# Two chained transformer blocks on one core: modulation chunks at other places, the Fourier sums taken token tile by token tile, first weight chunks in pieces

## The reference

```python
h  = modulate(rmsnorm(x, norm_mix_g[i]), sh1, sc1)       # h * (1 + sc1) + sh1
m  = fourier_mixer(h, w_fourier_out)                     # layer 0: real FFT over tokens and 256 features, then w_o
m  = retention_mixer(h, w_ret_in, w_ret_out, ...)        # layer 1
x  = x + g1 * m
h  = modulate(rmsnorm(x, norm_ffn_g[i]), sh2, sc2)
x  = x + g2 * (silu(h @ w_gate) * (h @ w_up)) @ w_out
...
mod = silu(c) @ w_ada[i] + b_ada[i]                      # gives sh1, sc1, g1, sh2, sc2, g2
out = modulate(rmsnorm(x, final_norm_g), shf, scf)
```

## Time and profile before

| | |
|---|---|
| median of 3 runs | 1191.15 us |
| the profiled execution's own time | 1189.39 us |
| its span, first to last instruction | 1187.2 us |
| mean granted TensorE clock | 0.991 |
| PE, DVE, ACT busy | 1146.8, 851.0, 521.0 us |
| DMA | 259.81 MB, mean 219 GB/s |

### The profile page before, as it was taken

The page is one execution under the profiler, slowest core; times in us unless marked ns, Lnnn a source line. Parts: engine busy times, 40 slices in busy tenths (PEclk is TensorE's granted clock), DMA queues, the critical chain, the costliest instruction groups (busy, mean ns, idle before and its releaser), DMA issues.

```text
span 1187.2 us, 13991 instructions
## 1 busy us (share of the span) xinstructions
PE 1146.8 (97%) x5824; PEld 965.3 (81%) x5824; DVE 851.0 (72%) x1009; ACT 521.0 (44%) x463; POOL 27.4 (2%) x51
## 2 busy tenths in 40 slices
PE   6999999999899999998999999999999999999996
PEld 5898998888688888877778888879976887888885
DVE  5789988986667677575657767478955867767755
ACT  5556555634444344444343434334423433434430
POOL 1000000000000000000000000000001000000000
PEclk8999999999999999999999999999999999999998
DMA  8754563547357768532357777448753563786761
GB/s 310 280 213 163 187 231 130 176 167 269 142 205 258 301 265 316 204 141 72 138 181 272 262 305 290 191 177 320 278 202 122 212 249 142 255 311 259 287 234 36
DMA packets 38638, 259.81 MB, mean 219 GB/s; under 512 B 4144, under 2 KB 6448, under 8 KB 7856
## 3 DMA queue, kind: packets, MB, share of 16 engines
q1 hardware_dynamic: 36960, 251.84, 57.0%
q0 software_dynamic: 1616, 7.08, 1.6%
HBM read 257.86 MB, written 1.05 MB: 218 GB/s over the span
## 4 chain that ended last, share of the span: by engine, by line
PE 85%; DVE 9%; issue 3%; ACT 2%; DMA 1%; POOL 0%; SPq 0%; DVEq 0%; POOLq 0%; ACTq 0%
PE pair L416 41%; PE pair L477 24%; PE pair L442 10%; DVE w_lo L1097 4%; PE tp L495 2%; PE tp L554 2%; DVE hb L1145 2%; PE tp L716 1%; PE tp L668 1%; DMA raw<-stream 1%; ACT w_hi L743 1%; PE tp L581 1%; ACT ht_hi L761 1%; PE tp L694 1%; DVE ht_lo L1157 1%
## 5 line engine op out<-in xcount | busy, mean ns | idle before, releaser
L1097 DVE TENSOR_TENSOR w_lo<-raw,w_hi 128x2048 fp32r<-128x2048 f32 x182 | 412.8, 2288 | 92.8 <-ACT w_hi L743 92.6
L743 ACT ACTIVATE w_hi<-raw 128x2048 fp32r<-128x2048 f32 x182 | 347.6, 1916 | 223.9 <-DMA raw<-stream 133.3
L416 PE MATMUL pair<-w_hi,ht_lo 128*128 128x512 f32 x816 | 327.9, 402 | 20.8 <-DVE w_lo L1097 12.2
L416 PE MATMUL pair<-w_lo,ht_hi 128*128 128x512 f32 x816 | 319.8, 392 | 0.0
L416 PE MATMUL pair<-w_hi,ht_hi 128*128 128x512 f32 x816 | 319.7, 392 | 0.0
L416 PEld LDWEIGHTS pair<-w_hi,ht_lo 128*128 128x128 f32 x816 | 154.3, 189 | 57.6 <-issue 14.7
L416 PEld LDWEIGHTS pair<-w_lo,ht_hi 128*128 128x128 f32 x816 | 154.2, 189 | 33.1
L416 PEld LDWEIGHTS pair<-w_hi,ht_hi 128*128 128x128 f32 x816 | 154.5, 189 | 31.3 <-issue 1.2
L477 PE MATMUL pair<-w_hi,gt_lo 128*128 128x512 f32 x360 | 142.3, 395 | 0.2 <-DVE gt_lo L1163 0.2
L477 PE MATMUL pair<-w_lo,gt_hi 128*128 128x512 f32 x360 | 140.3, 390 | 0.0
L477 PE MATMUL pair<-w_hi,gt_hi 128*128 128x512 f32 x360 | 140.1, 389 | 0.0
(11 more groups left out here) (201 smaller groups left out, 1101.8 us busy)
## 6 DMA issues: line engine op xcount, KB each, us to landing
raw<-stream SPq DMA_DIRECT2D x238, 1024.0 KB, 4.9
xres<-x SPq DMA_DIRECT2D x2, 512.0 KB, 6.8
prow<-rows POOLq DMA_DIRECT2D x1, 1024.0 KB, 9.7
xres<-x POOLq DMA_DIRECT2D x2, 512.0 KB, 4.9
dt<-decay POOLq DMA_DIRECT2D x1, 1024.0 KB, 7.1
outT<-outb SPq DMA_DIRECT2D x4, 256.0 KB, 2.2
csr<-dft POOLq DMA_DIRECT2D x1, 768.0 KB, 4.4
crow<-rows POOLq DMA_DIRECT2D x1, 512.0 KB, 6.4
```

The costliest lines, as they stand in the source:

```text
L416: mm = pe.matmul(pair[use % 2][:, t, :], a[:, 4 * c + k, t * P:(t + 1) * P], b[:, w % WS, k * 512:(k + 1) * 512], start=(c == 0 and k == 0 ...
L743: sc.activation(w_hi[:, w % WS, :], raw[:, n % RAW, :], ACT.Copy).then_inc(hi_done, 1)
L1097: v.tensor_tensor(w_lo[:, w % WS, :], raw[:, n % RAW, :], whi32[:, w % WS, :], ALU.subtract).then_inc(raw_done, 1)
```

## The change

- **Modulation chunks.** `ADA_TICKS`: 0, 1, 2, 5, 17, 18, 20, 31, 33 become 6, 18, 20, 33, 34, 35; in down0 three (1, 3, 5) become six (1 to 6). The total stays 56.
- **Start.** Chunks 0 and 1 are split in four pieces each; chunk 0 is also loaded in four. Tile 1 of x is asked for before the chunk. PE takes zu chunk by chunk, both tiles, in pieces, with 4 more warming products; zv is then an ordinary `wide`. `crow`, `hgrow` and the masks are asked for after chunk 5's hi part; silu(c) and the copy of the masks come later.
- **Normalisations.** DVE scales the first half, ACT the second (four ACTIVATE of 128 x 128 with scale and bias from columns). PE waits for one half at a time. `lo` of one chunk stands between DVE's two halves; at norm1 a chunk's split is drawn ahead of the normalisation.
- **Fourier.** The token sums of tile 0 run as soon as its feature sums are split, those of tile 1 at the end; they add up in `pair` instead of `tp`. The transposes of tile 0 stand in the middle of a chunk of the product ahead (`between`).
- **End.** The columns for the last modulation are made before the last two tiles, whose halves go to DVE and ACT.

```diff
-ADA_TICKS = [0, 1, 2, 5, 17, 18, 20, 31, 33]
-ADA_TICKS += ffn_adas("ffn0") + [W0["down0"] + j for j in (1, 3, 5)]
+ADA_TICKS = [6, 18, 20, 33, 34, 35]
+ADA_TICKS += ffn_adas("ffn0") + [W0["down0"] + j for j in range(1, 7)]
...
-             ("rows0", 2, "row_copied"), ("norm2b", 2, "norm"), ("dft1b", 4, "split"), ("dft2", 4, "split"),
+             ("norm2b", 2, "norm"), ("rows0", 2, "row_copied"), ("dft1b", 4, "split"),
...
+            sp.dma_start(xres[:, 1, :], x[:, 1, :]).then_inc(x_in[1], 16)
             sp.dma_start(col[:], cols).then_inc(small_in, 16)
-            sp.dma_start(raw[:, 0, :], stream[0]).then_inc(landed[0], 16)
-            sp.dma_start(xres[:, 1, :], x[:, 1, :]).then_inc(x_in[1], 16)
+            for q in range(PIECES):
+                sp.dma_start(raw[:, 0, q * 512:(q + 1) * 512], stream[0][:, q * 512:(q + 1) * 512]).then_inc(first_in[q], 16)
...
-                sp.wait_ge(raw_done, n + 1 - RAW)
+                sp.wait_ge(raw_done, pieces_done(n - RAW))
...
-            pool.dma_start(crow[:], rows[4:5, :].to_broadcast([P, D])).then_inc(crow_in, 16)
             rsqrt(RQ["norm0"], 2)
-            pool.wait_ge(hi_done, 2)
...
+            pool.wait_ge(hi_done, pieces_done(5))
+            pool.dma_start(crow[:], rows[4:5, :].to_broadcast([P, D])).then_inc(crow_in, 16)
...
-                wait_split(split, 2)
                 for c in range(4):
                     wait_chunk(w + c)
+                    if c < 2:
+                        wait_split(split, c + 1)
                     if c % 2 == 0:
                         claim_pair(use + c // 2)
                     wide_part(w + c, use + c // 2, c % 2, 0)
                     if c == 2:
                         norm()
-                wait_split(split, 4)
                 for c in range(4):
+                    if c < 2:
+                        wait_split(split, 3 + c)
                     wide_part(w + c, use + c // 2, c % 2, 1)
...
+            def first_tile(t, half, ready, n):
+
+                pe.wait_ge(ready, n)
+                turn(tile_job("norm0", t, half), [xn[:, t, (4 * half + k) * P:(4 * half + k + 1) * P] for k in range(4)])
...
+            def first_part(c, t, after={}):
+
+                n = SPLIT[tile_job("norm0", t, c)] + 1
+                for k in range(4):
+                    piece = PIECES * c + k + 1
+                    if t == 0:
+                        pe.wait_ge(hi_done, piece)
+                    if k == 0:
+                        pe.wait_ge(t_hi, n)
+                    out = pair[USE["zu"] % 2][:, t, :]
+                    ki, tk, wk = 4 * c + k, slice(t * P, (t + 1) * P), slice(k * 512, (k + 1) * 512)
+                    pe.matmul(out, ht[0][:, ki, tk], w_hi[:, c, wk], start=(c == 0 and k == 0), stop=False)
+                    if t == 0:
+                        pe.wait_ge(raw_done, piece)
+                    pe.matmul(out, ht[0][:, ki, tk], w_lo[:, c, wk], start=False, stop=False)
+                    if k == 0:
+                        pe.wait_ge(lo_done, n)
+                    mm = pe.matmul(out, ht[1][:, ki, tk], w_hi[:, c, wk], start=False, stop=(c == 1 and k == 3))
+                    if k in after:
+                        after[k]()
+                if t == TT - 1:
+                    mm.then_inc(w_used, 1)
...
+            first_tile(0, 0, xn_half, 1)
+            keep_warm(4)
+            first_part(0, 0, after={0: next_halves})
+            first_part(0, 1, after={1: lambda: first_tile(1, 1, xn_done, 2)})
+            first_part(1, 0)
+            first_part(1, 1)
+            wide(W0["zv"], USE["zv"])
...
-                  after={(1, 0): turn_tile("tx", xres, 1, x_ready, 4),
-                         (1, 1): turn_tile("norm2", xn, 0, xn_done, 5)})
+                  between={(2, 1): turn_tile("norm2", xn, 0, xn_done, 5)},
+                  after={(1, 0): turn_tile("tx", xres, 1, x_ready, 4)})
...
+            features("dft1", 0)
+            wait_evac(pe, USE["pleg"])
+            wait_evac(pe, USE["pleg"] + 1)
+            tokens("dft1", 0, (0, 1))
+            turn_tile("norm2", xn, 1, xn_done, 6)()
+            tokens("dft1", 0, (2, 3))
+            gate_rows("rows0", 1)
+            wait_split("norm2b", 2)
+            features("dft1b", 1)
+            tokens("dft1b", 1, range(4))
             outer(W0["fo"], 4, USE["fo"], tiles(ht),
...
+            def norm_scaled(name, t, scale, shift, dst, half=1):
+
+                k = tile_job(name, t, half)
+                act.wait_ge(tp_done, k + 1)
+                if k in SPLIT:
+                    at_least(act, lo_done, SPLIT[k] - 1)
+                for m in range(4):
+                    f = 4 * half + m
+                    ins = sc.activation(dst[:, m * P:(m + 1) * P], tp[k % BANKS][:, m * P:(m + 1) * P], ACT.Identity,
+                                        scale=scale[:, f:f + 1], bias=0.0 if shift is None else shift[:, f:f + 1])
+                ins.then_inc(sem(RELEASE[k][0]), 1)
...
             norm_squares(RQ["norm0"], 0, 0)
-            split_hi(0)
-            norm_his("norm0", 0)
-            split_hi(1)
             norm_squares(RQ["norm0"] + 1, 1, 0)
+            for q in range(3):
+                hi_piece(0, q)
+            norm_hi("norm0", 0, 0)
+            hi_piece(0, 3)
+            first_scaled(0)
+            norm_hi("norm0", 1, 0)
+            for q in range(PIECES):
+                hi_piece(1, q)
+            norm_hi("norm0", 0, 1)
+            first_scaled(1)
+            norm_hi("norm0", 1, 1)
             for w in range(2, WS):
                 split_hi(w)
-            act.wait_ge(crow_in, 16)
-            sc.activation(crow[:], crow[:], ACT.Silu).then_inc(ca_done, 1)
-            norm_his("norm0", 1)
...
-                norm_his(name, 0)
+                norm_his(name, 0, scale, shift)
                 tick(w - 1)
...
             for t in range(TT):
                 post_squares(RQ["mix"] + 2 * t, t, w + 3, USE["wout"], 3)
-                if t == 0:
-                    tick(w)
+                tick(w + 2 if t else w)
                 norm_squares(RQ["mix"] + 2 * t + 1, t, 1 + t)
                 tick(w + 3 if t else w + 1)
-                norm_his("norm1", t)
-                if t == 0:
-                    tick(w + 2)
+                norm_his("norm1", t, colv("ffn_pre", 0, 8))
...
-            dft_his("dft1b", 1, range(4))
-            for gr in range(4):
-                k = JOB["dft2"] + gr
-                hi(k, ht[0][:, 2 * gr:2 * gr + 2, :], _two(tp[k % BANKS][:], k))
-                if gr != 2:
-                    tick(w - 2 + (gr + 1) // 2)
-            boundary(W0["fo"] + 3, RQ["norm3"], "norm3", 7)
+                norm_his("norm2", t, moda[:, 0, :], mod[:, 0:8])
+            gate_rows("rows0", grow[0])
+            dft_his("dft1b", 1, (0, 1, 2))
+            tick(w - 2)
+            dft_his("dft1b", 1, (3,))
...
+            def mix_his(groups):
+                for gr in groups:
+                    act.wait_ge(mix_done, gr + 1)
+                    sc.activation(ht[0][:, 2 * gr:2 * gr + 2, :], mixed(gr).rearrange("p (a b) -> p a b", a=2),
+                                  ACT.Copy).then_inc(mix_hi, 1)
+
+            mix_his((0, 1))
+            tick(w - 1)
+            mix_his((2, 3))
+            tick(w)
```

More of the change, by code:

```diff
@@ L146, with tile_job, pieces_done @@
 USE, JOB, RELEASE, SPLIT = plan_psum()
-def tile_job(name, t):
-    return JOB["norm2b"] if name == "norm2" and t else JOB[name] + 2 * t
+def tile_job(name, t, half=0):
+    if name == "norm0":
+        return JOB[name] + 2 * half + t
+    return (JOB["norm2b"] if name == "norm2" and t else JOB[name] + 2 * t) + half
+PIECES = 4
+FINE = 2
+def pieces_done(n):
+    return n + 1 + (PIECES - 1) * min(n + 1, FINE)
 RQ = {}
@@ L257, in program @@
         landed = [sem(f"landed{i}") for i in range(RAW)]
+        first_in = [sem(f"first_in{q}") for q in range(PIECES)]
+        xn_half = sem("xn_half")
         raw_done = sem("raw_done")
@@ L474, in outer @@
                     for half in range(2):
+                        if half and (c, t) in between:
+                            between[c, t]()
                         for k in range(2):
@@ L673, in _ @@
+            features("dft1", 0)
[8 more added lines that the diff above has]
+            tokens("dft1b", 1, range(4))
             outer(W0["fo"], 4, USE["fo"], tiles(ht),
-                  before={(c, 0): lambda c=c: wait_split("dft2", c + 1) for c in range(4)},
+                  before={(c, 0): lambda c=c: pe.wait_ge(mix_lo, max(c + 1, 2)) for c in range(4)},
@@ L916, in boundary @@
                 tick(w)
-                norm_his(name, 1)
+                norm_his(name, 1, scale, shift)
             def gated_chunks(half, name0, plan):
```

244 lines of the change are left out of this document (147 added, 97 removed).

## The result

The changed kernel takes 1176.76 us, median of 4 runs (1175.15 to 1178.84), beside 1190.62 us before in the same comparison (1189.44 to 1191.34): a ratio of 0.9886, 95% interval 0.9864 to 0.9907, so 1.1% faster. Run again beside other kernels it took 1178.01 (1174.04 to 1178.24), ratio 0.9884 (0.9866 to 0.9902). The forecast was 1175.0, with 1173.3 for a profiled execution; the profiled one took 1175.15 (span 1173.1), 14.2 less than before, where 16.1 were forecast.

A forecast was written before the change was run, and what follows sets the result against it. TensorE, busy 97% of the span, bounds the kernel; with the same products only its idle time can change. Terms -6.6 + 6.1 + 2.2 - 4.1 - 6.8 - 6.3 - 0.6 = -16.1 take 1191.15 to 1175.0 us, range 1170 to 1180 (1167 to 1184 with rivals).

The forecast's parts named there:

- down0: Six modulation chunks in a row in down0: chunk 74 ready before needed, so 0 lost, bounds 0 and 5 us.
- the rival, whose mechanism is what happened: down0 stalls too: with landings up to 6.6 us six pairs lose 6.3 less the lead's 1.2, giving 1180; 8%.
- wa and wout: Two modulation chunks ahead of merge(1) make TensorE wait for its tile: 6.1 us lost, bounds 2.5 and 9.
- The clock behind it: Half clock for 3.4 to 5.3 us after the wait at wa: 2.2 us lost, bounds 0 and 2.7.
- The start: Up to qa: first product near 11.2, qa near 36 instead of 42.71, 6.6 us gained, bounds 3 and 8.
- the second rival: Start and clock gains fall short: tile 1 lands late and holds both tiles, half clock lasts longer; 1181, 17%.
- norm1: Joint behind wout: tile 1's products start at 319.0 instead of 323.2, 4.1 us taken as gain, bounds 2.4 and 4.5.
- norm3 to norm5: Three joints, first gap gone and tile 1's products sooner: 2.1 us gained each, 6.3 in all, bounds 1 and 2.6 each.
- Fourier: Fourier stage: token sums of tile 0 fill idle time, fo starts at 552.8, 6.8 us gained, bounds 4 and 7.
- ScalarE's scaling: Second halves scaled on ScalarE: 1.1 us for four, or 1.6 with about 93 ns per column operand.
- the end: After the last transposes, scaling shared by VectorE and ScalarE: 0.6 us gained, bounds 0 and 0.9.

The follow-up runs named there:

- down_spaced: Changed kernel with three modulation chunks in down0 (ticks 1, 3, 5) instead of six in a row, the others at ticks 17, 19, 31: 1175.44 us.
- both_free: Changed kernel with seven modulation chunks before down0, five in it (ticks 1, 3, 4, 5, 6), none at ticks 34 and 35 in wa: 1166.42 us.
- wa_free: Changed kernel with its first six modulation chunks at ticks 6, 17, 18, 20, 31, 33, none at ticks 34 and 35 in wa: 1168.60 us.
- merge_first: Changed kernel with merge(1) one place earlier on VectorE, ahead of the tick that holds the split of chunk 40: 1172.97 us.
- wa_warm: Changed kernel with 18 warming products on TensorE in the stall ahead of the transposes of ga tile 1: 1176.22 us.
- scale_first: Changed kernel with VectorE scaling and splitting tile 0's first half before tile 1's power -1/2 at the start: 1175.67 us.
- crow_early: Changed kernel with crow (512 KB) asked for at once by GpSimd's queue, as before the change: one execution, 1176.59 us.
- dve_scales: Changed kernel with both halves of the scaling on VectorE again in norm1 to norm5: 1179.23 us.

## Why the prediction was right, point by point

- **The total.** 1175.0 forecast, 1176.76 and 1178.01 measured, inside 1170 to 1180. By the medians 13.9 were gained instead of 16.1. In the one execution that was profiled the sum is off by 1.9. One term, down0, makes 1.8 of it. The others are off by 0.2 to 0.6 each, and that they cancel to within 0.2 is luck.
- **down0, the term that failed.** It was put at 0: 5.6 us a pair against 5.45, chunk 74 ready 1.2 before it is needed. That took 4.7 us for every landing, the median of the earlier trace rows. With an item freed every 2.3 us, several loads are under way at once; those asked for at 454.7 to 459.7 took 5.8, 6.3 and 6.8, and the `w_lo` behind them started at 462.42 and 468.44, 7.9 and 6.0 after the one before. The next two pairs took 5.5 and 5.9, their loads 4.7 to 5.0. That this shows at the last chunk lies in `outer` too: it goes through the last four chunks for tile 0 first, 12 products (2.72 us) each, and then for tile 1. By the starts of products and the ends of `w_lo`:

| chunk | `w_lo` ends | TensorE is there | lead |
|---|---|---|---|
| 70 | 456.84 | 467.04 | 10.2 |
| 71 | 464.71 | 472.48 | 7.8 |
| 72 | 470.74 | 475.20 | 4.5 |
| 73 | 476.28 | 477.92 | 1.6 |
| 74 | 482.17 | 480.64 | -1.5 |

  So most of the lead goes in these four, as it did before (11.2 at chunk 71, 3.7 at chunk 74), and 0.15 a chunk does not describe it. The need was forecast rightly (483.7, which is 480.6 here, 3.1 being gained by then); the chunk was ready 2.8 later than forecast. The 6.6 of the earlier trace rows was used only for the rival, whose mechanism is what happened, at 1.8 instead of 5.1. Over the ten profiled executions with six chunks in a row the step was 1.4 to 3.1, never 0, and it was largest (3.1) in the two whose slowest load there took 7.6 and 7.9; among the other eight (6.4 to 7.4, a step of 1.4 to 2.2) there is no clear order. down_spaced and both_free take it away.
- **wa and wout.** Right in kind: 5.5 instead of 6.1, because chunk 40 landed 4.9 after it was asked for, where the prediction took 5.7. wa_free, merge_first and wa_warm show the order, the landing and the clock apart.
- **The clock behind it.** 1.8 instead of 2.2 in the first profile. Over the eight executions with this stall the slow products alone cost 0.7 to 2.1, with the transposes 1.4 to 2.9; four of the eight lie above the term's upper bound of 2.7. By the Trainium skill (TensorE: Matmul & The Clock Gate, What's actually happening) activity is what releases the full rate; wa_warm agrees: warming products, whose results nobody uses, kept it at 1.00.
- **The start.** 6.1 instead of 6.6. First product 11.36 (11.2 forecast), half clock 3.4 us (3 forecast), which cost 1.3 to 1.7 (1.5 to 2 forecast). The cause was split wrongly: crow is worth about 3, not 1.2. That tile 1 would land late and hold tile 0, the second rival, did not happen: it landed at 6.93, and scale_first gains nothing by its order. In crow_early tile 1 and the columns both land 3 us later and the first product with them, so the rival was a real possibility; which of the two held it there is not separated.
- **norm1, norm3 to norm5, Fourier.** 4.3, 2.0 each and 6.5, within 0.3 of the terms. At norm1 the clock happened to stay; in 7 of the 12 profiled executions with that gap it fell, at a cost of 1.4 to 1.6 us. That is one reason why the medians lie above the first profile.
- **ScalarE's scaling, a price that was too low.** Forecast 1.1 us for four with scale and shift. It is 1.1 with a scale alone and 1.5 with both:

```profile
L860 ACT ACTIVATE hb<-tp,mod,moda 128x128 f32<-128x128 f32 x32 | 11.9, 451 | 0.0
L860 ACT ACTIVATE hb<-tp,col 128x128 f32<-128x128 f32 x16 | 4.5, 365 | 2.8 <-PE tp L528 2.8
```

  The forecast took the 592 and 1024 ns of the earlier trace rows as times from start to start; they are the durations of single instructions. By the same line a 128-element one without columns would last 0.27 (an estimate). With a scale from a column it lasts 0.365, with both 0.451: 0.09 for each column operand. The Trainium skill (ScalarE: Activation LUTs, What ACT_TABLE_LOAD costs) has 93 ns for each, and the trace agrees for both. In a row they overlap: 4.5 / 16 is 0.28 from start to start, 11.9 / 32 is 0.37, inside the prediction's bounds of 0.17 to 0.6. The price that the prediction gave beside its sum, 1.6 for four, was the better one, and it named the right places. In the Fourier stage TensorE waits 0.4 behind ScalarE's four, dve_scales takes 0.3 less there, and the term was 6.5 instead of 6.8. At the end the gain was 0.3 instead of 0.6: ScalarE's four begin at 1168.95 and take 1.50, VectorE's had ended at 1169.47.

## What to carry to other kernels

A ring's period is not its best landing time: work it out with the landing of several loads under way, and chunk by chunk against the times at which the consumer takes them, since its last chunks may be taken twice as fast as the others. Space small items that empty a buffer quickly, or put them where the engine that uses them is not about to release the busiest one. Before hoisting work into an engine's written order, look at what stands behind it, and at the load that its successor in the ring will wait for. Keep an instruction's duration apart from the time between two starts: on ScalarE they differ by 0.08 us here. Idle time of TensorE is best priced with and without the clock behind it; where it can't be removed, filling it with products is cheap and steadies the time.
